# Experts' results by indirect transfers of GpSimd to a row per token and slot, read back by SyncE

## The reference, cut to what matters

```python
# top_i, top_w: 8 experts of each token and their weights
rows, wts, blk_expert = ...        # assignments sorted by expert, each expert padded to blocks of 128
def one_block(rb, e):
    g, u = split(t_pad[rb] @ w_gu[e])          # 128x1024 by 1024x512
    return (silu(g) * u) @ w_dn[e]             # 128x256 by 256x1024
ys = one_block for every block
out[rows] += ys * wts                          # back to the tokens
x = x + g2 * (out + shared); rmsnorm(x)
```

## Time and profile before

| | us |
|---|---|
| median of 3 runs | 3437.49 (3436.98 to 3439.31) |
| profiled execution | 3437.43 |
| its span, first to last instruction | 3435.6 |
| TensorE busy | 3298.7 (96%) |
| VectorE busy | 1999.6 (58%) |
| ScalarE busy | 1769.2 (51%) |
| GpSimd busy | 1209.7 (35%) |

### The profile page before, as it was taken

One profiled execution on the slowest core, in us unless ns is written; L12 is line 12 of the kernel. 1 busy time (PEld: TensorE's weight loads), 2 busy tenths in 40 slices (PEclk: granted clock), 3 DMA queues, 4 the chain that ended last, 5 costly groups with the idle time before them and its releaser, 6 DMA issues.

```text
span 3435.6 us, 48285 instructions
## 1 busy us (share of the span) xinstructions
PE 3298.7 (96%) x16320; PEld 2645.7 (77%) x16320; DVE 1999.6 (58%) x2489; ACT 1769.2 (51%) x2130; POOL 1209.7 (35%) x625
## 2 busy tenths in 40 slices
PE   8999999999999999999999999898899999999996
PEld 6888887778888788888678888687666788887783
DVE  4335674653353433631563333558866799888887
ACT  5552325455524555221645533424563688888883
POOL 3444441144444444444044444343102222222224
PEclk9999999999999999999999999999899999999998
DMA  3225321022253223533322233222002899999997
GB/s 123 98 98 168 113 98 47 26 92 96 93 169 125 81 96 98 168 113 116 111 85 92 97 98 98 79 92 84 25 7 94 338 403 412 411 414 406 395 398 306
DMA packets 128099, 555.34 MB, mean 162 GB/s; under 512 B 19344, under 2 KB 19600, under 8 KB 100112
## 3 DMA queue, kind: packets, MB, share of 16 engines
q1 hardware_dynamic: 112896, 520.59, 41.5%
q0 software_dynamic: 14976, 33.58, 2.6%
q10 hardware_dynamic: 144, 0.08, 0.0%
HBM read 531.62 MB, written 41.94 MB: 167 GB/s over the span
## 4 chain that ended last, share of the span: by engine, by line
PE 61%; issue 25%; POOL 8%; DVE 5%; ACT 1%; DMA 0%; POOLq 0%; DVEq 0%; ACTq 0%
PE ps L752 17%; PE ps L754 16%; PE ps L753 16%; POOL w_lo L1792 7%; PE ps L1210 2%; PE ps L772 1%; PE ps L913 1%; PE ps L1289 1%; PE ps L938 1%; PE ps L923 1%; PE ps L1039 1%; PE ps L1021 1%; PE ps L1000 1%; PE ps L963 0%; PE ps L1229 0%
## 5 line engine op out<-in xcount | busy, mean ns | idle before, releaser
L1792 POOL TENSOR_TENSOR w_lo<-stage_buf,w_hi 128x1024 fp32r<-128x1024 f32 (+1 forms) x396 | 972.2, 2455 | 1513.3 <-ACT w_hi L1365 1513.3
L1365 ACT ACTIVATE w_hi<-stage_buf 128x1024 fp32r<-128x1024 f32 (+1 forms) x396 | 414.0, 1046 | 1192.6 <-PE ps L754 1144.3
L752 PE MATMUL ps<-x_hi,w_hi 128*128 128x512 f32 x1984 | 776.4, 391 | 8.8 <-POOL w_lo L1792 7.9
L753 PE MATMUL ps<-x_lo,w_hi 128*128 128x512 f32 x1984 | 774.7, 390 | 0.0
L754 PE MATMUL ps<-x_hi,w_lo 128*128 128x512 f32 x1984 | 774.6, 390 | 0.0
L752 PE MATMUL ps<-hid,w_hi 128*128 128x512 f32 x1312 | 518.9, 396 | 2.7 <-issue 1.7
L754 PE MATMUL ps<-hid,w_lo 128*128 128x512 f32 x1312 | 511.6, 390 | 0.0
L753 PE MATMUL ps<-hid,w_hi 128*128 128x512 f32 x1312 | 510.8, 389 | 0.0
L752 PEld LDWEIGHTS ps<-x_hi,w_hi 128*128 128x128 f32 x1984 | 374.3, 189 | 90.4 <-POOL w_lo L1792 9.6
L754 PEld LDWEIGHTS ps<-x_hi,w_lo 128*128 128x128 f32 x1984 | 374.1, 189 | 78.6
L753 PEld LDWEIGHTS ps<-x_lo,w_hi 128*128 128x128 f32 x1984 | 374.4, 189 | 77.3
(11 more groups left out here) (398 smaller groups left out, 4886.6 us busy)
## 6 DMA issues: line engine op xcount, KB each, us to landing
stage_buf<-in_gu SPq DMA_DIRECT2D x176, 512.0 KB, 3.2
big<-in_exp_gu SPq DMA_DIRECT2D x72, 1024.0 KB, 13.4
h_buf<-in_exp_gu SPq DMA_DIRECT2D x72, 1024.0 KB, 13.4
s_buf<-in_exp_dn SPq DMA_DIRECT2D x72, 1024.0 KB, 13.5
slot_rows<-stage_buf SPq DMA_DIRECT2D x72, 512.0 KB, 13.1
stage_buf<-in_down SPq DMA_DIRECT2D x64, 512.0 KB, 3.6
stage_buf<-in_down SPq DMA_DIRECT2D x32, 384.0 KB, 3.2
sil_buf<-in_ada SPq DMA_DIRECT2D x24, 512.0 KB, 4.2
```

The costliest lines, as they stand in the source:

```text
L752: nc.tensor.matmul(o, a_hi, b_hi, start=start, stop=False)
L753: nc.tensor.matmul(o, a_hi, b_lo, start=False, stop=False)
L1365: nc.scalar.activation(w_hi[s][:, 0:n], stage[s][:, 0:n], ACT.Copy).then_inc(upper_done, 1)
L1792: nc.gpsimd.tensor_tensor(w_lo[s][:, 0:n], stage[s][:, 0:n], w_hi[s][:, 0:n].bitcast(F32), ALU.subtract).then_inc(parted, 1)
```

## The change

`slot_rows` is laid out by token and slot instead of by block and place: tile, token, slot, 1024 elements. SyncE's `store_rows` is removed. GpSimd gets a `scatter` for each block: it waits for the evacuation (`bk["oev"]`), casts the block's column of a second table `tab_v`, and sends the evacuated rows by an indirect transfer to row 8 x token + slot; empty places are out of bounds and skipped. In the loop it stands behind the gather of the block three further on. The table is filled with the pair's number (token and slot) instead of the token's: VectorE compares and scales in 32 short operations (ScalarE's four scalings and the cast to `slot_i` are removed), and three more chained operations derive the token's number from the pair's. The evacuation's first two turns wait for no transfer, for which ScalarE's first turn of the loop is written out. GpSimd's 32 indirect fetches are removed; SyncE makes 32 plain requests for the same rows, 4 KB each at a stride of 32 KB, behind its last weight loads. A few waits on counts move with this.

```diff
-        slot_no, tok_no = mask[:, 704:705], mask[:, 705:709]
-        BLOCKS, NO_ROW = MAX_BLOCKS + 4, 4096
-        tab_f, FAR = mask[:, 1024:1024 + BLOCKS], 16384
+        slot_no, pair_no = mask[:, 704:705], mask[:, 705:737]
+        BLOCKS, FAR = MAX_BLOCKS + 4, 16384
+        tab_f, tab_v = (mask[:, a:a + BLOCKS] for a in (1024, 1024 + BLOCKS))
...
-                    def store_rows(i, s):
-                        sp.wait_ge(bk["oev"], i * 2 + (s + 3))
-                        sp.dma_start(dr["slots"][bass.ds(i * 2 + s, 1), :, :].rearrange("a p n -> p (a n)"), o_sb[s].bitcast(I32)
-                                     ).then_inc(o_out[s], 16)
                     with sp.Fori(0, more) as i:
                         for s in range(2):
                             load_down(i, s)
                             e = expert_of(bass.ds(i * 2 + (s + 4), 1))
                             sp.wait_ge(raw_parted[0], i * 2 + (s + 3))
                             load_raw(e, s, 0)
-                            store_rows(i, s)
                             sp.wait_ge(raw_parted[1], i * 2 + (s + 3))
                             load_raw(e, s, 1)
                     for s in range(2):
                         load_down(more, s)
-                        store_rows(more, s)
+                    def fetch(row, t, k, done):
+                        sp.dma_start(row.bitcast(I32), dr["slots"][t, :, k, :]).then_inc(done, 16)
+                    def after(done, n):
+                        sp.wait_ge(done, n)
+                        sp.sem_inc(bk["waited"], 1)
                     for s in range(2):
-                        store_rows(more + 1, s)
+                        after(o_out[s], more * 16)
+                    for k in range(EARLY):
+                        if k == 2:
+                            after(bk["gu"], more * 2 + 4)
+                        elif k == 3:
+                            after(bk["dn"], more * 2 + 4)
+                        for t in range(TT):
+                            if k < 2 and t % 2 == 0:
+                                after(raw_parted[t // 2], more * 2 + (3 + k))
+                            fetch(rows[k * TT + t], t, k, row_in[k])
+                    for i, (t, k) in enumerate(LATE):
+                        if i == 0:
+                            for s in range(2):
+                                after(o_out[s], more * 16 + 16)
+                            after(o_out[0], more * 16 + 32)
+                        if k == 7 and t == 0:
+                            after(o_out[1], more * 16 + 32)
+                        sp.wait_ge(fin["row"], max(i, k == 4 and 4 * t) + 1)
+                        fetch(rows[i], t, k, row_last[t] if k == 7 else row_in[t])
...
-                    pe.wait_ge(tab["scaled"], t + 1)
...
-                    for t in range(TT):
-                        act.wait_ge(tab["pairs"], t + 1)
-                        nc.scalar.activation(at_b[t], at_b[t], ACT.Copy, scale=tok_no[:, t:t + 1]).then_inc(tab["scaled"], 1)
...
-                    def evacuate(s, i):
+                    def evacuate(s, i, first=False):
                         act.wait_ge(bk["dn"], i * 2 + (s + 2))
-                        act.wait_ge(o_out[s], i * 16 + 16)
+                        if not first:
+                            act.wait_ge(o_out[s], i * 16)
...
+                    two_blocks(0, first=True)
+                    with act.Fori(1, more_n + 1) as i:
+                        two_blocks(i)
...
+                    def scatter(s, b, n):
+                        pool.wait_ge(bk["oev"], n + 2)
+                        nc.gpsimd.tensor_copy(out_idx[:, s:s + 1], tab_v[:, b]).then_inc(bk["placed"], 1)
+                        pool.wait_ge(bk["placed"], n)
+                        pool.sem_inc(bk["asked"], 1)
+                        nc.gpsimd.indirect_dma_start(
+                            out=dr["slots"].rearrange("t p k n -> (t p k) n"),
+                            out_offset=bass.IndirectOffsetOnAxis(ap=out_idx[:, s:s + 1], axis=0),
+                            in_=o_sb[s].bitcast(I32), in_offset=None,
+                            bounds_check=T * TOP_K - 1, oob_is_err=False).then_inc(o_out[s], 16)
                     with pool.Fori(0, more_n) as i:
                         for s in range(2):
                             pool.wait_ge(bk["tx"], i * 2 + (s + 2))
                             gather(1 - s, bass.ds(i * 2 + (s + 3), 1), i * 2 + (s + 4))
+                            scatter(s, bass.ds(i * 2 + s, 1), i * 2 + (s + 1))
                     pool.wait_ge(bk["tx"], more_n * 2 + 2)
                     gather(1, bass.ds(more_n * 2 + 3, 1), more_n * 2 + 4)
-                    def fetch(row, t, k, done):
-                        pool.sem_inc(bk["asked"], 1)
-                        n = t * TOP_K + k
-                        nc.gpsimd.indirect_dma_start(
-                            out=row.bitcast(I32), out_offset=None, in_=dr["slots"].rearrange("b p n -> (b p) n"),
-                            in_offset=bass.IndirectOffsetOnAxis(ap=slot_i[:, n:n + 1], axis=0)).then_inc(done, 16)
...
-                        fetch(rows[i], t, k, row_last[t] if k == 7 else row_in[t])
+                    for j in range(4):
+                        scatter(j % 2, bass.ds(more_n * 2 + j, 1), more_n * 2 + (j + 1))
...
-                    nc.vector.tensor_tensor(at_b[t], iota_t[:, None, 0:BLOCKS].to_broadcast([P, TOP_K, BLOCKS]),
-                                            slot_b[:, c, None].to_broadcast([P, TOP_K, BLOCKS]), ALU.is_equal
-                                            ).then_inc(tab["pairs"], 1)
+                    for k in range(TOP_K):
+                        n = t * TOP_K + k
+                        ins = nc.vector.tensor_scalar(at_b[t][:, k, :], iota_t[:, 0:BLOCKS], slot_b[:, n:n + 1], pair_no[:, n:n + 1],
+                                                      ALU.is_equal, ALU.mult)
+                    ins.then_inc(tab["pairs"], 1)
...
-                nc.vector.tensor_scalar(tab_f, ps[:, 6, 0:BLOCKS], float(NO_ROW), None, ALU.add).then_inc(tab["in"], 1)
+                link(nc.vector.tensor_scalar(tab_v, ps[:, 6, 0:BLOCKS], float(2 * T * TOP_K), None, ALU.add))
+                link(nc.vector.tensor_scalar(tab_f, tab_v, 1.0 / TOP_K, 0.5 / TOP_K - 0.5, ALU.mult, ALU.add))
+                link(nc.vector.tensor_scalar(tab_f, tab_f, 12582912.0, None, ALU.add))
+                nc.vector.tensor_scalar(tab_f, tab_f, -12582912.0, None, ALU.add).then_inc(tab["in"], 1)
...
-                             number, number + P * np.arange(TT, dtype=np.float32) - 4096], axis=1)
+                             number, (TOP_K * (number[:, :, None] + P * np.arange(TT, dtype=np.float32)[None, :, None])
+                                      + np.arange(TOP_K, dtype=np.float32) - 2 * T * TOP_K).reshape(P, TT * TOP_K)], axis=1)
...
-    dr["slots"] = nc.dram_tensor("slot_rows", [MAX_BLOCKS, P, D], I32, kind="Internal").ap()
+    dr["slots"] = nc.dram_tensor("slot_rows", [TT, P, TOP_K, D], I32, kind="Internal").ap()
```

More of the change, by code:

```diff
@@ L462, in block_kernel @@
         slot_r, slot_b, slot_w = (pt_buf[:, 1920 + 32 * j:1952 + 32 * j] for j in range(3))
[L463 removed]
+        slot_f = small[:, 0:32]
         ssq, sdev, sinv = small[:, 64:68], small[:, 68:72], small[:, 72:76]
@@ L1274, in sum_rows @@
                     if t == 0:
-                        pe.wait_ge(tab["scaled"], TT + 1)
+                        pe.wait_ge(tab["scaled"], 1)
                     pe.wait_ge(row_in[t], 64 + 48)
```

35 lines of the change are left out of this document (6 added, 29 removed).

## The result

| | before | after |
|---|---|---|
| median, us | 3438.40 (3436.98 to 3440.90) | 3678.54 (3671.87 to 3685.31) |
| profiled execution, span | 3435.6 | 3670.0 |
| mean granted clock of TensorE | 0.981 | 0.958 |

The changed kernel is slower by 7%: the ratio is 1.0695, with an interval of 1.0682 to 1.0708. I had forecast 3498 us and a range up to 3560. The sign was right, but 60.9 us were forecast and 240 came: the size was four times too small, and the range missed. (Brackets behind a time are its lowest and highest run, behind a ratio its 95% interval.)

A forecast was written before the change was run, and what follows sets the result against it. The prediction took the loop to be bound by TensorE, with the DMA engines at its heels. Loop +64.7, tables +0.7 and tail -4.5 made +60.9 us on 3437.43, so 3498 us, with a range of 3438 to 3560.

The forecast's parts named there:

- The mechanism: GpSimd's loop: the gather behind the scatter starts 11.5 us later against 7.3 of slack, stalling TensorE's transposes; +64.7 us.
- Let each round be stalled by d: Loop: every round gets the same stall d, taken as 1.1 us (bounds 0.2 to 2.1), over 67 rounds.
- E: Loop: time from the end of a gather's transfer to its landing, taken as 3.2 to 5 us, bounds 1.5 to 7.4.
- the free case: Loop: VectorE's subtraction doesn't hold the gather's transfer, which ends at 6.3 us; d = (E - 3.18) / 2.
- TensorE's clock: Loop: a fall of the granted clock in the stalls, named only as a sign that the prediction is wrong; no size.
- A: Rival, loop: gathers still land slowly, E 6.3 to 7.4, d 1.6 to 2.1; 3530 to 3565 us; chance 0.2.
- B: Rival, loop: gathers land quickly behind another transfer, d 0.2 to 0.7; 3438 to 3471 us; chance 0.19.
- C: Rival, loop: faster; VectorE's subtraction holds up neither cast nor transfer and the gather is in time; 3425 us; chance 0.13.
- the caught formula: Loop: the subtraction holds the gather's transfer until 7.2 + d, so d = E - 2.28; with its cast caught too, E - 1.28.
- D: Rival, tail: plain read-back requests or row writes run well below today's rate, adding 10 to 40 us; about 3530; chance 0.03.
- Tables: Ahead of the loop: short comparisons hide in VectorE's idle time, three chained operations cost 3 x 0.23 = +0.7 us.
- Tail: After the loop: SyncE's plain requests land the third late row at 3393.5 instead of 3398.1; -4.5 us.

The follow-up runs named there:

- e1: The changed kernel with the next gather issued ahead of the scatter, a buffer turn earlier; 3428.21 us, ratio 0.9968 to the kernel before.
- e8: The changed kernel with each of VectorE's 128x2048 subtractions made as four of 128x512; 3566.34 us.
- e6: The changed kernel with weight loads of half the columns, so the experts' results are wrong; 3515.85 us.
- e7: The changed kernel with the scatter's bound at row 0, so nearly all its rows are skipped, and the read-back taking rows of the tokens; 3616.21 us.
- e3: The changed kernel with 40 transposes of the identity on TensorE every second round, ahead of its wait for the late gather; 3621.29 us.
- e2: The changed kernel with the scatter's cast made ahead of the wait for the evacuation, order scatter then gather kept; 3653.94 us.
- e4: The kernel before with one added line: GpSimd waits for block n's evacuation ahead of the gather of block n+4; 3527.61 us, ratio 1.0263.
- e9: e1 with the scatter's cast ahead of the wait for the evacuation and VectorE's 128x2048 subtractions as two of 128x1024; 3431.04 us, ratio 0.9972.
- e5: e1 plus a SyncE store of 0.29 MB per block in pieces of 2304 bytes, to a buffer nobody reads; 3474.64 us, ratio 1.0103.
- e10: e1 plus a SyncE store of 0.29 MB per block in pieces of 3584 bytes, to a buffer nobody reads; 3471.10 us, ratio 1.0089.

## Why the prediction missed

**The mechanism: right in its kind.** The gather behind the scatter comes 11.5 us later against 7.3 of slack, and TensorE waits for it; e1 shows that nothing else in the loop costs time. The times within a round were right to 0.1 us. Predicted for a caught gather was a transfer that ends 8.2 us after the nominal start of the round when the cast is caught, and at 6.3 when it is free: measured 3017.52 - 3009.28 = 8.24, and 3025.10 - 3018.76 (where the round would have begun without its stall) = 6.34.

**The step that failed first: "Let each round be stalled by d".** I looked for one stall that repeats itself. But its own offsets say how one round's stall follows from the last one's (E is the time from a gather's transfer to its landing). From no stall, the subtraction catches the cast, and the next stall is 8.2 + E - 9.48 = E - 1.28. From a long stall the gather is free, and the next is 6.3 + E - 9.48 less the stall itself: nothing. So they alternate between E - 1.28 and 0, and a pair takes 18.96 + E - 1.28. The equal stall is where I stopped; a second round worked from the first would have shown that it isn't reached. In e8, where the gather is hardly held, the stalls fall on both buffers, and by the free case its pair should be 18.96 + 7.0 - 3.18 = 22.8: measured 23.15, which is in part luck, since 0.76 us of a slower clock stand against 0.5 of an earlier transfer.

**The term that was mis-sized: E.** I let the backlog drain and took 3.2 to 5 us; it is 6.50 at the mean for the gathers that TensorE waits for, by the weights in transit and the scatter's rows, which I had given nothing (e6, e7). The best row, the 7.4 us of the earlier trace rows, I had set aside for the quieter ones. The mean rate was no guide: the loop moves 285 and 269 GB/s, less than the 341 that I had worked out, but the DMA share is 0.87 in the round in which this gather is under way and 0.58 in the next.

**What was missing: TensorE's clock.** The prediction named its fall as something that would make it wrong, and gave it no case and no price. It falls behind the long stalls, and takes 1.84 us a pair. Among the long stalls the length hardly shows: behind 9.9 us the round took 11.1 us at a granted clock of 0.83, behind 4.7 us 12.2 at 0.75.

Predicted were 2 x 10.58 = 21.16 us a pair, measured 26.32. Over 67 rounds, 33.5 pairs, with 4.1 us for the E that I had assumed:

| step | us per pair | in all |
|---|---|---|
| stalls alternate (18.96 + 4.1 - 1.28 = 21.78) | 0.62 | 21 |
| E 6.5 instead of 4.1 | 2.40 | 80 |
| granted clock (12.32 - 10.48) | 1.84 | 62 |
| rest: start of transfer 0.09, transfer 0.09, landing to turn 0.12 | 0.30 | 10 |

That is 173 of the 176 us by which the loop missed (+240.7 against +64.7); e3's 57 us for the clock agrees with its line. How the first two lines share their 101 us depends on the order: with E = 6.5 the equal stall alone would have been 1.66 us and the sum 3536, so the alternation is worth 21 us at the E that I had assumed and 64 at the one measured. From 3498 to 3679 it is 180 us; in the profiled execution, 3671.87 us, the stages ahead of the change happened to be 4.5 us shorter, and the tail gained 1.8 less than predicted.

**The rivals.** A, the slow landing, was the nearest, and its E of 6.3 to 7.4 contains the one measured. Its 3530 to 3565 us were too small for the same two reasons, the equal stall and the clock. B and C fell: with the transfer free the gather would still land late. C's ground, that VectorE's subtraction holds up neither cast nor transfer, is contradicted by the 1.92 us of the cast and the 2.78 us of e2's transfer, and by e8, where short subtractions are worth over 100 us. The Trainium skill (SBUF — State Buffer, Who interferes with whom) infers only that a `tensor_tensor` leaves descriptor writing alone; here the indirect transfer as a whole is held, and whether by the reading of its row list or by the writing of its descriptors no run tells. The 2.5 us that I worked out from the Trainium skill (DMA: Bandwidth & Descriptors, Anatomy of one DMA — SWDGE (gpsimd) path) is the least that a gather of the earlier trace rows took from its issue; as an E it was too low by far, with 2.9 and 3.3 us at the mean even in e6. (By the caught formula it would have given d = 0.22 and 3439 us, not 0.25 and 3441.) D didn't happen.

**The other parts.** Tables: +0.7 predicted, +0.9 measured. The eight short comparisons of a tile:

```profile
2642.28 2.02 DVE L2535 TENSOR_SCALAR big<-mask,pt_buf 128x100 f32<-128x100 f32 x8
```

They take 2.0 to 2.5 us where one of 128x800 took 0.98, and hide as predicted. The weights' waits are gone, as said. Tail: -4.5 predicted, -2.7 measured, and for another reason. The rows of after:

```profile
3614.84 1.56 POOL L1886 DMA_INDIRECT slot_rows<-stage_buf,mask  x1 [0.87 <-POOL mask L1883]
...
3617.48 1.02 ACT L1766 ACTIVATE stage_buf<-ps 128x1024 f32<-128x1024 f32 x1 [3.59 <-PE ps L777]
...
3632.66 9.61 PE L1301 MATMUL ps<-big,tmp_buf 128*128 128x512 f32 x16 [15.22 <-DMA big<-slot_rows]
```

The sums start 15.2 us after the last evacuation begins, not 9. Block 70's scatter lands 9.7 us after 3614.84, which is 8.1 behind its transfer where I had put 6, and the late requests wait for that. The third of them goes out at 3625.43, behind one that waits until 3625.12 for an addition of VectorE, and lands 7.1 us later, as the chain of waits has it:

```profile
3625.43 7.10 DMA big<-slot_rows
```

What the tail gains, it gains ahead of the evacuation: from the last block's turn to the end of its evacuation it is 24.2 us instead of 28.2, and in the kernel before ScalarE had waited 4.24 us for the last weights, a wait that is gone:

```profile
3373.97 1.91 ACT L1763 ACTIVATE hid<-s_buf 128x2048 fp32r<-128x2048 f32 x1 [4.24 <-DMA s_buf<-in_exp_dn]
```

## What to carry to other kernels

Where a step on an in-order queue gets a new wait, look at what stands behind it: a prefetch that has slack belongs ahead of a store that must wait, and here that order is worth 250 us of 3679. Where a stall comes back through a loop, work two or three rounds forward from the first, each with its own offsets, instead of solving for one that repeats; and where TensorE's stalls grow long (5.4 us at the mean here; not the 1.5 us of e4), add the rounds at the lower granted clock to the bill. For a latency take the row under the load that the change leaves, and count what the change puts on the same queue.

## What the runs showed of the hardware

- After stalls of some 6.6 us TensorE's granted clock was 0.80 over the next round, which took 11.49 us of unbroken work instead of 9.48. 40 transposes without use in the stall kept it at 0.98 to 1.00. In e4, whose stalls are 1.5 us at the mean and 3.3 at most, it was 0.98.
- A cast of GpSimd that starts inside a 128x2048 subtraction of VectorE doesn't end before it: all 232 of them in after and e1 end 0.04 to 0.05 us behind it (1.92 to 2.10 us instead of 0.19 where it had just begun). An indirect transfer that starts inside one ends some 0.9 us behind it (2.78 instead of 1.03 in e2). Two of 128x1024 still bring a transfer to 1.82 (e9); with four of 128x512 the casts inside one took 0.55 at the median and the gathers' transfers 1.05 (e8).
- A gather of 0.23 MB at the mean landed 4.3 us after its issue (medians) with half of the weights in transit, 5.4 with all of them but no rows of a scatter ahead of it, 6.7 with both and 8.4 with the DMA engines full.
- Engines with a DMA share of 1.00 moved 406 to 414 GB/s in the kernel before and 382 to 397 in e1, e5 and e10, where a larger part is GpSimd's (13.5% of their time in e1, 6.6% before). That the mix is the reason wasn't tested by itself.
